# Forgetting attention of a hybrid decoder block: key blocks transposed, copied and split in pairs

## The reference, cut to what matters

```python
def fox_attention(q, k, v, log_f):
    scale = D ** -0.5
    c = cumsum(log_f)                                  # over tokens, per head
    def one_block(qb, cb, start):                      # 128 queries
        s = einsum('bhqd,bhkd->bhqk', qb, kh) * scale
        s = s + cb[..., :, None] - c[..., None, :]
        p = softmax(where(key_pos <= q_pos, s, -inf), axis=-1)
        return einsum('bhqk,bhkd->bhqd', p, vh)
```

## Time and profile before

| what | value |
|---|---|
| runs | 1271.3, 1272.03, 1273.73 us |
| the profiled execution: its own time, its span | 1274.2 us, 1272.5 us |
| TensorE busy over the span (matmul records) | 1218.3 us, 96% |
| VectorE, ScalarE, GpSimd busy | 661.4, 547.5, 407.7 us |
| transposes of the changed stage (line 1797) | 816, 133.2 us |
| ScalarE copies of transposed blocks (1867) | 240, 124.1 us |
| VectorE low parts (1923) | 240, 143.9 us |
| VectorE negations (1912) | 240, 141.5 us with their accumulator reads |
| ScalarE exponentials (1859) | 96, 114.8 us with their accumulator reads |

### The profile page before, as it was taken

How to read it: one execution, slowest core, us unless ns; L and a number is a source line. 1 busy time by engine, 2 the same in 40 slices (tenths; PEclk the granted TensorE clock), 3 DMA queues, 4 the chain that set the end, 5 groups by cost and what they waited for, 6 DMA issues and landing times. The chain is left out here.

```text
span 1272.5 us, 18832 instructions
## 1 busy us (share of the span) xinstructions
PE 1218.3 (96%) x6256; PEld 997.8 (78%) x6256; DVE 661.4 (52%) x1496; ACT 547.5 (43%) x1116; POOL 407.7 (32%) x512
## 2 busy tenths in 40 slices
PE   5999999999999999998999989989999998899997
PEld 5998877888777777777888767877787787688886
DVE  3763435101333334423555369878898887544443
ACT  5553133013444442213555357777787777211111
POOL 3553631122333333323334143252225315111110
PEclk9999999999999999999999989999999999799999
DMA  8884132223333334435444493235045201443431
GB/s 317 265 288 130 62 96 97 72 82 115 101 107 107 107 107 132 130 120 155 131 150 141 125 229 121 91 97 140 9 150 114 70 10 57 192 149 149 149 146 70
DMA packets 106820, 161.57 MB, mean 127 GB/s; under 512 B 12148, under 2 KB 62324, under 8 KB 105124
## 3 DMA queue, kind: packets, MB, share of 16 engines
q1 hardware_dynamic: 103920, 151.46, 38.1%
q10 hardware_dynamic: 2616, 8.66, 1.7%
q0 software_dynamic: 192, 0.33, 0.2%
HBM read 102.67 MB, written 57.74 MB: 126 GB/s over the span
## 5 line engine op out<-in xcount | busy, mean ns | idle before, releaser
L1038 PE MATMUL tok_tps<-h_T,tok_slot 128*128 128x512 f32 x2088 | 489.8, 392 | 0.0
L1038 PEld LDWEIGHTS tok_tps<-h_T,tok_slot 128*128 128x128 f32 x2088 | 389.6, 188 | 82.6 <-issue 2.3
L2104 PE MATMUL out_yps<-out_w,out_mix 128*128 128x512 f32 x768 | 178.3, 395 | 7.9 <-POOL out_mix L2153 7.1
L2104 PEld LDWEIGHTS out_yps<-out_w,out_mix 128*128 128x128 f32 x768 | 146.1, 191 | 40.4 <-ACT out_w L2170 8.5
L1867 ACT ACTIVATE fox_pT<-fox_tps 128x512 fp32r<-128x512 f32 x240 | 124.1, 529 | 80.8 <-PE fox_tps L1797 77.4
L1923 DVE TENSOR_TENSOR fox_pT<-fox_tps,fox_pT 128x512 fp32r<-128x512 f32 x240 | 143.9, 606 | 20.3 <-ACT fox_pT L1867 18.3
L1912 DVE TENSOR_SCALAR_CACHE_REDUCE fox_prob<-fox_sps 128x512 f32<-128x512 f32 (+1 forms) x240 | 141.5, 605 | 11.4 <-PE fox_sps L1788 9.3
L1797 PE MATMUL fox_tps<-all_ident,fox_prob 128*128 128x128 f32 x816 | 133.2, 276 | 4.6 <-ACT fox_prob L1859 3.0
L1797 PEld LDWEIGHTS fox_tps<-all_ident,fox_prob 128*128 128x128 f32 x816 | 101.7, 141 | 31.9 <-ACT fox_prob L1859 6.3
L1859 ACT ACTIVATE fox_prob<-fox_prob,fox_nm 128x512 f32<-128x512 f32 (+7 forms) x96 | 114.8, 1196 | 5.5 <-POOL fox_qb L1567 5.3
L1814 PE MATMUL fox_ops<-fox_pT,fox_v 128*128 128x512 f32 (+3 forms) x384 | 112.2, 375 | 1.6 <-ACT fox_pT L1867 1.6
(11 more groups left out here) (199 smaller groups left out, 1671.0 us busy)
## 6 DMA issues: line engine op xcount, KB each, us to landing
scr_split<-cg_stage SPq DMA_DIRECT2D x64, 256.0 KB, 2.9
open_raw<-in_w_cols SPq DMA_DIRECT2D x22, 512.0 KB, 4.4
open_raw<-in_x SPq DMA_DIRECT2D x16, 512.0 KB, 6.6
tok_xT<-in_x_cols SPq DMA_DIRECT2D x16, 512.0 KB, 6.2
scr_gates<-cg_stage SPq DMA_DIRECT2D x32, 256.0 KB, 2.5
outw_mix<-scr_mix SPq DMA_DIRECT2D x16, 512.0 KB, 4.4
out_x<-in_x SPq DMA_DIRECT2D x16, 512.0 KB, 3.5
out<-out_o ACTq DMA_DIRECT2D x15, 512.0 KB, 2.6
```

The costliest lines, as they stand in the source:

```text
L1038: mm = nc.tensor.matmul(cps[u % 2], w[j % 2][a_][:, kk, :], hT[b_][:, kk, c * CH:(c + 1) * CH], start=(kk == 0 and r == 0), stop=(kk == KT ...
L2104: mm = nc.tensor.matmul(yps[t % 2][:, c, :], mix[t % 2][a][:, kk, :], w[b][:, kk, c * CH:(c + 1) * CH], start=(kk == 0 and n == 0), stop=( ...
```

## The change

1. A step handles a pair of key blocks j, j + 1. `key_units` yields pairs; a turn has 2(g + 1) steps in place of 4(g + 1). `plan` is unchanged and spreads the same score units and exponentials over half as many steps.
2. `tps` becomes two buffers of two banks each (was three of one). The transposes of both blocks are issued together, with one signal after the last. The condition for the first is that the pair before the previous one has its low part.
3. `pt_high` and `pt_low` take both blocks of a pair in one instruction of 1024 columns where the pair lies wholly before the diagonal (`stretches`); in the two pairs on the diagonal they are two instructions, with one signal.
4. Two buffers of pairs for the high and low parts; a pair is weighed one step after its transposes (all high products first, then all low ones).
5. `rps` is now `sps[0]`, so `spread_sums` also waits until the scores in flight are negated (all but the last unit, which lies in the other bank), and the first score of a turn waits until `scale` has been copied out.
6. For g = 0 the reduction over one column goes: the negation writes its minimum into `nm` at once, and the exponential waits for `negated`.
7. `invert` moves behind the first `pt_low` of its turn. `ends` for a turn of two steps is its second.

```diff
     def key_units(hd, g):
-        for j in range(4 * (g + 1)):
+        for j in range(0, 4 * (g + 1), 2):
             yield hd, g, j, max(0, j - 4 * g)
+    def blocks(u):
+        hd, g, j, i0 = u
+        return [(b, j + b, max(0, j + b - 4 * g)) for b in range(2)]
+    def stretches(u):
+        hd, g, j, i0 = u
+        return [(slice(0, 2), 0)] if j < 4 * g else [(slice(b, b + 1), first) for b, _, first in blocks(u)]
...
-        pT = [[k.sb(f"pT{b}{i}", [P, CH], F32R) for i in (HI, LO)] for b in range(PT)]
+        pT = [[k.sb(f"pT{b}{i}", [P, 2, CH], F32R) for i in (HI, LO)] for b in range(PAIRS_KEPT)]     # PAIRS_KEPT = 2
-        tps = [k.ps(f"tps{b}", [P, CH]) for b in range(3)]
+        tps = [k.ps(f"tps{b}", [P, 2, CH]) for b in range(2)]
-        rps = k.ps("rps", [P, CH])
+        rps = sps[0]
...
-            return t >= 1 and m == (len(list(key_units(*turns[t])))-2)
+            return t >= 1 and m == max(len(list(key_units(*turns[t]))) - 2, 1)
...  TensorE, scores
+                        if n >= QT and i == QT - 1 and c == 0:
+                            turn = next(x for x in range(n_turns + 2) if starts(x) == n) - 1
+                            pe.wait_ge(scaled, G.at(max(turn - 1, 0)))
...  TensorE, transposes
-                        pe.wait_ge(pt_lo, K.at(n - 2 if n >= 3 else 0))
-                        for i in reversed(range(i0, QT)):
-                            if q0:
-                                pe.wait_ge(expd, E.at(QT * t + QT - i))
-                            mm = nc.tensor.transpose(tps[n % 3][:, i * P:(i + 1) * P],
-                                                     prob[t % 2][:, i, j * P:(j + 1) * P], ident[:, :])
+                        pe.wait_ge(pt_lo, K.at(n - 1 if n >= 2 else 0))
+                        for b, jb, start in blocks(u):
+                            for i in reversed(range(start, QT)):
+                                if q0 and b == 0:
+                                    pe.wait_ge(expd, E.at(QT * t + QT - i))
+                                mm = nc.tensor.transpose(tps[n % 2][:, b, i * P:(i + 1) * P],
+                                                         prob[t % 2][:, i, jb * P:(jb + 1) * P], ident[:, :])
...  TensorE, spread_sums
+                        pe.wait_ge(negated, S.at(starts(min(t + 3, n_turns + (not last))) - 1))
...  TensorE, the turn
-                            if len(waiting) > DEPTH:
+                            if len(waiting) > 1:
                                 weigh(*waiting.pop(0))
...  ScalarE, pt_high (pt_low on VectorE likewise)
-                        act.wait_ge(weighed, K.at(max(n - PT + 1, 0)))
-                        nc.scalar.activation(pT[n % PT][HI][:, i0 * P:CH], tps[n % 3][:, i0 * P:CH], ACT.Copy
-                                             ).then_inc(pt_hi, 1)
+                        act.wait_ge(weighed, K.at(max(n - PAIRS_KEPT + 1, 0)))
+                        for b, start in stretches(u):
+                            mm = nc.scalar.activation(pT[n % PAIRS_KEPT][HI][:, b, start * P:CH],
+                                                      tps[n % 2][:, b, start * P:CH], ACT.Copy)
+                        mm.then_inc(pt_hi, 1)
...  VectorE, negate
-                                                ALU.mult, ALU.min, accum_out=nmax[t % 2][:, i, c:c + 1]
+                                                ALU.mult, ALU.min,
+                                                accum_out=nmax[t % 2][:, i, c:c + 1] if g else nm[t % 2][:, i:i + 1]
                                                 ).then_inc(negated, 1)
-                        if c == g:
+                        if c == g and g:
...  VectorE, the turn
-                        invert(t)
                         for m, (u, made, _) in enumerate(steps):
                             for a in made:
                                 negate(ahead[a], s1 + a, t + 1)
                             pt_low(u, k0 + m)
+                            if m == 0:
+                                invert(t)
```

More of the change, by code:

```diff
@@ L1643, in forgetting_attention @@
         heads = (first, second)
+        PAIRS_KEPT = 2
         prob = [k.sb(f"prob{b}", [P, QT, T]) for b in range(2)]
-        pT = [[k.sb(f"pT{b}{i}", [P, CH], F32R) for i in (HI, LO)] for b in range(PT)]
+        pT = [[k.sb(f"pT{b}{i}", [P, 2, CH], F32R) for i in (HI, LO)] for b in range(PAIRS_KEPT)]
         nmax = [k.sb(f"nmax{b}", [P, CH // P, 4]) for b in range(2)]
@@ L1669, in forgetting_attention, with maxima_before @@
         n_turns = len(turns)
+        def maxima_before(t):
+            return sum(QT * (g > 0) for _, g in turns[:t])
         def at_turn(t):
@@ L1673, in at_turn, with starts @@
                     sum(len(list(key_units(*x))) for x in turns[:t]))
+        def starts(t):
+            return (t // n_turns) * n_scores + at_turn(t % n_turns)[0]
         def plan(t, last):
@@ L1813, in weigh @@
                                 pe.wait_ge(pt_lo, K.at(n + 1))
-                            mm = nc.tensor.matmul(ops[t % 2][:, i0 * P:CH], heads[e].value(j), pT[n % PT][i][:, i0 * P:CH],
-                                                  start=(first and i == HI), stop=(last and i == LO),
-                                                  skip_group_check=True)
+                            for b, jb, start in blocks(u):
+                                mm = nc.tensor.matmul(ops[t % 2][:, start * P:CH], heads[e].value(jb),
+                                                      pT[n % PAIRS_KEPT][i][:, b, start * P:CH],
+                                                      start=(first and i == HI and b == 0),
+                                                      stop=(last and i == LO and b == 1), skip_group_check=True)
                         mm.then_inc(weighed, 1)
@@ L1853, in round_ @@
                 def round_(r, last, prologue=False):
-                    K, G, E = Ring(r, n_keys), Ring(r, n_turns), Ring(r, QT * n_turns)
+                    S, K, G = Ring(r, n_scores), Ring(r, n_keys), Ring(r, n_turns)
+                    M = Ring(r, maxima_before(n_turns))
                     def exponentials(t, i):
                         w = keys_of(turns[t % n_turns][1]) - (CH - P * (i + 1))
-                        act.wait_ge(maxed, E.at(QT * t + QT - i))
+                        if turns[t % n_turns][1] == 0:
+                            act.wait_ge(negated, S.at(at_turn(t)[0] + QT - i))
+                        else:
+                            act.wait_ge(maxed, M.at(maxima_before(t) + QT - i))
                         nc.scalar.activation(prob[t % 2][:, i, 0:w], prob[t % 2][:, i, 0:w], ACT.Exp,
@@ L1922, in pt_low @@
                         dve.wait_ge(pt_hi, K.at(n + 1))
-                        nc.vector.tensor_tensor(pT[n % PT][LO][:, i0 * P:CH], tps[n % 3][:, i0 * P:CH],
-                                                pT[n % PT][HI][:, i0 * P:CH].bitcast(F32), ALU.subtract
-                                                ).then_inc(pt_lo, 1)
+                        for b, start in stretches(u):
+                            mm = nc.vector.tensor_tensor(pT[n % PAIRS_KEPT][LO][:, b, start * P:CH],
+                                                         tps[n % 2][:, b, start * P:CH],
+                                                         pT[n % PAIRS_KEPT][HI][:, b, start * P:CH].bitcast(F32), ALU.subtract)
+                        mm.then_inc(pt_lo, 1)
                     def invert(t):
```

## The result

The changed kernel takes 1316.86 us (median of four runs, 1316.17 to 1318.5) against 1272.88 us for the kernel before on the same chip: ratio 1.035, 95% interval 1.0337 to 1.0363, 44 us slower. The profiled execution took 1317.36 us by its own time, its span is 1315.6. The forecast had the sign and less than half of the size: +18 where it is +44, and 1317 lies outside its range.

What follows compares the result with a forecast made beforehand. Bound by VectorE in t1 to t3's dense parts with ScalarE tails, TensorE in t4 to t6, engine chains in t0 and t7. Turn changes of 5.95 us a round gave +18: 1274.2 to 1292, forecast 1290 us, range 1271 to 1303.

Steps and rivals of the forecast that it cites:

- the tails: End of a turn, set by ScalarE's chain; later last exponentials were to lengthen t2 by 2.5 us, t1 1.6, t3 1.0.
- the walk: Step-by-step timing of the changed turns from instruction prices; in t2 the dense part ends at 14.6 us, the tail takes 7.0.
- The sum: All turns' predicted changes added: 5.95 us slower a round, 17.9 for three rounds, taken as +18.
- a score unit 0.5: Price in us that the timing of turns gave TensorE for one score unit, read from starts in the earlier trace.
- The clock: Rival: idle TensorE in t2's tail drops its clock, adding 6 to 10 us, 1299 in all; chance 0.24.
- that wait costs nothing by itself: In t3 the first score's new wait for `scale` ends at 21.65 us, before the last low part at 22.85.
- t5, priced 0: Turn where TensorE is always busy; copies and low parts were to fit without a stall, so no change.
- t6, priced 0: Turn with a full TensorE, judged the same way as t4: no stall, so no change.
- t7, priced +0.35: Short turn: four exponentials ahead of `low_half` and a second spread waiting for `scale`, +0.35 us net of the reductions saved.
- the rival of savings alone: Tails no later, only VectorE's joining and reduction savings count: 7.4 to 10.3 us less, 1264; chance 0.15.
- the low end was 0.08: Lower bound in us of VectorE time saved per joined low part, of 0.08 to 0.16, over 72 joins.
- a wash: Rival: timing right in sign but too dark in size, savings and later turn ends cancel, 1272 us; chance 0.09.

Runs made afterwards that it cites:

- e2: Changed kernel, but a step may also take the exponentials of tiles whose scores it deals itself: 1291.06 us, ratio 1.0135.
- e11: Changed kernel with early exponentials and, in bunches of three or four score units, the third and fourth behind the weighing: 1283.72 us, ratio 1.0076.
- e13: e1 with a third score bank and the spread sums put into a score bank: 1330.21 us, ratio 1.0445.
- e1: Kernel before, with scores and exponentials dealt once per two key blocks; no wide instructions, pair buffers or shared bank: 1335.7 us, ratio 1.0492.
- e7: Changed kernel with 20 unread identity transposes ahead of the first transposes of turns t1 to t4: 1315.34 us, ratio 1.0335.
- e8: Kernel before, with only the spread sums moved into the first score bank and the two waits that go with it: 1278.65 us, ratio 1.0043.
- e9: Kernel before without the 24 reductions for g = 0, the negation writing its minimum itself: 1273.53 us, ratio 0.9999.
- e14: e11 with every copy and low part of 512 columns a separate instruction again: 1286.59 us, ratio 1.0108.
- e6: Changed kernel with every pair copied and split by two instructions of 512 columns instead of one of 1024: 1320.52 us, ratio 1.0366.
- e12: e9 plus the line of e2 allowing earlier exponentials, at the grain of blocks: 1297.23 us, ratio 1.0183.

## Why the prediction was wrong

**Right.** Slower, and for the greater part by the tails. ScalarE's chain in t2 took 6.26 us against 6.35 in the walk, and putting the exponentials back (e2) returned 26 of the 44 us, the falls of the clock among them. Joined copies took 1026 ns and joined low parts 1221 ns (forecast 1.03 and 1.21 us), with 1.14 from start to start (forecast 1.12):

```profile
L1956 DVE TENSOR_TENSOR fox_pT<-fox_tps,fox_pT 128x1024 fp32r<-128x1024 f32 x72 | 87.9, 1221 | 0.3
...
L1897 ACT ACTIVATE fox_pT<-fox_tps 128x1024 fp32r<-128x1024 f32 x72 | 73.8, 1026 | 92.2 <-PE fox_tps L1819 92.2
```

t4 came out as forecast (-0.2), and TensorE waits for the exponential for 3 us in t2.

**Wrong, by the steps.** The sum was 5.95 us a round and the turns say 14.9. Of the 8.9 missed, 3.0 lie in t2, 1.7 in t1, 1.5 in t3, 0.8 each in t5 and t6, 0.7 in t7 and 0.4 in t0.
- "a score unit 0.5" is the step that failed first. The earlier trace rows show units that stand in a queue. The walk dealt four at once to two banks and still let VectorE go from negation to negation at 0.61. From its start to its negation a unit that finds TensorE empty takes 0.77. The walk falls behind by 0.3 to 0.6 us a step, and t2's dense part is 16.55 in place of 14.6: 1.95 of the 3.0 us missed in t2. Where half of a large bunch stands behind the weighing (e11) it is 15.40, and VectorE idles 0.92 us of it in place of 1.81; a third bank took 2 us off it in the kernel with coarse dealing (e13 against e1).
- The clock was a rival, with 6 to 10 us, and not in the sum. It falls seven times in the stage, after 3.04 us of idle TensorE in the case shown, and costs an estimated 6 us (e7). It comes on top of the forecast, not in its place; in t2 it is most of the tail's 8.1 us in place of 7.0 (7.2 in e7).
- "that wait costs nothing by itself" held where it was said: in t3 of the changed kernel the wait is 0.2 us. The 4.9 us of the shared bank stand in the kernel before (e8). t5, priced 0, is 0.8 longer in both kernels; why isn't shown.
- t6, priced 0, is 0.8 longer; with early exponentials it is 8.19 again. Its four exponentials stand in fewer steps too, and I had excused it because TensorE is full there.
- t7, priced +0.35, is +1.05. The mechanism was right, four exponentials ahead of `low_half` and a second spread that waits for `scale`, and its size wrong: `scale` ends 1.2 us later than before and the spread starts 0.56 us later. The other 0.5 us are the transposes of a pair ahead of the first score: seven in 0.94 us, before four in 0.36.
- The reductions, counted with 4.5 us in the rival of savings alone: nothing (e9). Joining took 0.06 us a join off VectorE's busy time where the low end was 0.08.

**The account** by differences of experiments on the way back: late exponentials and the clock falls that come with them 27 us (after to e2, by the ratios; 26 by the medians), bunches of three and four 7.5 (e2 to e11, by the ratios). What is left is e11's 10 us over the kernel before; joining had taken off about 4 by then (e14), so some 14 us come from the pair grain, the shared bank and the moved `invert` in ways that no run separates. t2's dense part in e11 still has 0.8 us more of idle VectorE than before and its busy time 0.4 more.

**Open.** Why e1 is 18 us slower than the changed kernel, although it lacks the shared bank: joining explains about 4; the rest (e1 puts a bunch between the transposes of two blocks, and shows more low clock) wasn't tried. And e13's loss in t4 and t5.

**Rivals and the rule.** Savings alone and a wash are out. Of the two sentences of the Trainium skill, "Perfetto Trace Analysis", section "Optimizing Scalar/DVE Operations", the first was borne out in sign: grouping saved about 4 us of busy time on each of the two engines and about 4 us of time (e14). The second, on breaking instructions up, was not, although the prediction laid the loss to it: with the joined instructions broken up again no time came back (e6, e14), and the kernel that loses most (e1) has no larger instruction than before. What cost was the size of the steps, by their dealing: 27 and 7.5 us (e2, e11). The page's section "Optimization Strategy" says that consistent bubbles can mean that PSUM or SBUF is short of room for the next tile. TensorE's waits of 0.32, 0.59 and 0.34 us before the third score unit in t2's first three steps were such bubbles, and with a third bank the like waits in e1 went from 4.0 to 0.4 us of weight loads (e13).

## What to carry to other kernels

Halving the number of steps of a software pipeline also doubles what each step deals to the other engines, even if the rule of dealing stays word for word the same. Before joining instructions, compare the bunch with the number of its buffers, and the place of every item on the critical chain with the item that it used to precede. If instructions are to be joined, try to keep dealing in the old grain; no run here did, and what joining can win is about 4 us. A rule of when an item may be issued is tuned to one grain: the same line was worth -26 us at one and +24 at the other.

## What the runs showed that I had not expected

- A score unit of two matmuls of 512 columns takes 0.77 us from start to the start of its negation if TensorE was empty, against 0.5 from unit to unit in a queue; with two buffers the two engines then work in turn.
- 24 reductions of 0.155 us on the engine that looked fullest were worth nothing (0.9999, 0.999 to 1.0008).
- Exponentials placed a step too early cost as much as exponentials placed a step too late: 24 us in the kernel with blocks (e12), 26 in the one with pairs (e2), there with the falls of the clock.
- A bank shared by two uses cost 4.9 us in the kernel with blocks (e8, 8.5 us of waits), and in the kernels with pairs its wait all but vanishes (0.7 and 0.9 us).
